# First expert tile in four lots beside the second tile's input projection

## The chip, the cores and the metric

One core of one Trainium2 chip runs the whole program. The metric is the device time of one execution in microseconds. The kernel before takes 2155.31 us, the median of three runs (2154.33 to 2156.59).

## The reference, cut to what matters

A model of two blocks works on 256 tokens of width 1024, in float32. The first block has two layers. Each layer is a mixer (attention) followed by a feed-forward part that retrieves experts by product keys, a chunk of 128 tokens at a time:

```
q = (xc @ w_q).reshape(t, PEER_HEADS, 2, PEER_QDIM // 2)
sc = jnp.einsum('thpc,hpnc->thpn', q, sub_keys)
v_half, i_half = lax.top_k(sc, 16)
cand = v_half[:, :, 0, :, None] + v_half[:, :, 1, None, :]
top_s, pos = lax.top_k(cand.reshape(t, 8, -1), 16)
g = softmax(top_s)
act = gelu(einsum('thkd,td->thk', u_tab[expert], xc))
out = einsum('thk,thkd->td', g * act, v_tab[expert])
```

Each token picks 8 heads x 16 = 128 experts. Each expert is a row of u and a row of v, 8 KB together. With 128 tokens on 128 partitions, one pick (say, head 3, rank 5) of all tokens is one gather of 1 MB. There are 128 such gathers for each tile of 128 tokens and each layer, 512 in all. The second block has four kinds of attention, gates and an MLP, and gathers nothing.

## The kernel before, in words

The tokens are two tiles of 128. The program is a list of stages. `stage` (L273) adds one, and `run_stages` (L278) has PE, ACT and DVE run their part of each and meet at its end (the wait at L289). The stages of the first layer are: the mixer of tile 0 (`hybrid(0)`), the feed-forward norm, turn and routing of tile 0 (`feed_forward(0, [0], enter_hybrid, halved=True)`, L1643), the mixer of tile 1, and the feed-forward of tile 1.

Routing (`route`, L1319) has three steps. PE makes the queries in four blocks of 512 columns (L1359). ACT copies them out (L1383). PE multiplies each block with the keys of two heads (L1348), and ACT copies the scores out (L1378). DVE then finds the 16 best of each of 16 score lists (`top16`, L1403, rounds of MAX8, FIND_INDEX8 and MATCH_REPLACE8) and, in `select` (L1431), combines the two halves of each head, takes the 16 best pairs and turns their places into expert numbers (L1436 to L1488). For tile 0 of the first layer this runs in two lots of four heads (`halved`), and the first lot's numbers go to POOL before the second lot is sorted. The softmax over the picks is a subtraction on DVE (L1503), an exp on ACT (L1393) and three DVE instructions (L1506 to L1508), once for all heads, at the end of the stage.

Beside that routing, after the query blocks and key scores, PE runs the input projection of tile 1 (`enter_hybrid`, L1198): eight transposes (L1216), and six column blocks in two halves each (L494). Its first four column blocks read weights that were kept in SBUF since tile 0. Those eight kept pieces lie in the eight slots of the ring into which the gathers land, so gather n (n below 8) waits until PE has read piece n (L2611). ACT empties the blocks (L1038).

POOL issues the gathers in order (L2596 to L2615). From the ninth on, each waits until the slot's last use is over (`freed`, L1576).

The work on a gathered row is an item (`start_experts`, L1514). For item i, DVE takes the dot product of row i with the token (L1530). ACT makes gelu (L1546), the weight (L1547) and a diagonal matrix (L1555) of item i-1. PE adds row i-2 into `ps_acc` with two matmuls (L1566, four records), or DVE adds it (L1538), which `share_out` decides by the kind of the stage. Items are not a stage of their own: they are handed out at the `point`s of other stages (L256). Each point has a weight, and `handed_out` (L251) gives out items in proportion to the weight passed, so that 122 of the 128 are out when the next tile's routing ends:

```
return f["first"] + int(weight * min((P - HELD_BACK - f["first"]) / max(f["weight"], 1.0), RATE))
```

For the first tile's items, the points run from the rotations of tile 1 to the end of tile 1's routing. Their weights by stage are: rotations 25, turn 6, index 31, attention 53, turn 3, output projection 14.9, norm 9, turn 3, routing 92.5.

SP issues the weight loads in the order of `stream` (L2566 to L2577), each after the use that frees its slot of four.

## Time and profile before

| | us |
|---|---|
| median of three runs | 2155.31 |
| the profiled execution | 2154.64 |
| span of its trace | 2152.8 |
| outside the span | 1.8 |

| engine | busy us | share of the span |
|---|---|---|
| PE | 1669.8 | 78% |
| DVE | 1487.4 | 69% |
| ACT | 797.5 | 37% |
| POOL | 641.7 | 30% |

The span runs from the first instruction to the last. All positions below are us from its start. An engine's row in a timeline names the line, the operation, the output and inputs, and in brackets how long the engine was idle before and what ended the wait. Some fp32 matmuls show as two records.

### The profile page before, as it was taken

How to read it: one execution, taken by the hardware profiler on the slowest of the kernel's cores; microseconds unless marked ns; L12 is line 12 of the kernel's file. 1: busy time of each engine (PE TensorE's matmuls, PEld its weight loads, DVE VectorE, ACT ScalarE, POOL GpSimd, SP SyncE). 2: the span in 40 equal slices, each digit the busy share in tenths (PEclk: the TensorE clock that was granted, in tenths of full speed). 3: DMA queues.
4: the chain of work that ended last, by engine and by line, in shares of the span. 5: the costliest groups of instructions: out<-in, count | busy, mean ns of one | idle time of the engine just before them, and what ended most of it. 6: DMA issues, size and time to landing. Idle time of an engine off the chain costs nothing.

```text
span 2152.8 us, 20655 instructions
## 1 busy us (share of the span) xinstructions
PE 1669.8 (78%) x6494; PEld 1007.3 (47%) x6494; DVE 1487.4 (69%) x3088; ACT 797.5 (37%) x2066; POOL 641.7 (30%) x524
## 2 busy tenths in 40 slices
PE   8797777577767775777777487756777899898998
PEld 4573343522324353333344332544333465668986
DVE  4378867897666669876667897668777464566654
ACT  1213452234424322432452145113545343444542
POOL 0012444344433443543344364335454000000000
PEclk9999889889898887998889799887888999999999
DMA  7368999999999999999999999999999774474552
GB/s 273 144 233 349 398 392 421 419 419 422 415 421 388 401 421 389 418 420 421 396 381 414 385 399 422 420 421 421 367 413 406 302 279 173 176 293 147 181 191 98
DMA packets 105659, 745.29 MB, mean 346 GB/s; under 512 B 12880, under 2 KB 13520, under 8 KB 16720
## 3 DMA queue, kind: packets, MB, share of 16 engines
q0 software_dynamic: 73728, 536.90, 60.9%
q1 hardware_dynamic: 31248, 204.98, 24.7%
q10 hardware_dynamic: 576, 2.10, 0.3%
q8 instruction: 53, 0.87, 0.2%
q14 instruction: 54, 0.44, 0.1%
HBM read 742.89 MB, written 1.05 MB: 346 GB/s over the span
## 4 chain that ended last, share of the span: by engine, by line
PE 41%; DMA 21%; DVE 20%; ACT 10%; issue 6%; DVEq 1%; PEldq 1%; POOL 0%; PEld 0%; ACTq 0%; SPq 0%; POOLq 0%
DMA sb_work<-in_peer_uv,sb_expert 17%; PE ps_acc L1566 12%; PE bank L494 6%; DVE sb_work L1530 5%; PE bank L1359 4%; DVE sb_x L1538 3%; PE bank L2054 2%; DMA sb_wring<-in_peer_w_q 2%; ACT L1546 2%; PE bank L564 2%; PE ps_acc L564 2%; PE ps_acc L565 2%; PE ps_acc L566 2%; PE bank L775 2%; PE bank L565 2%
## 5 line engine op out<-in xcount | busy, mean ns | idle before, releaser
L2612 POOL DMA_INDIRECT sb_work<-in_peer_uv,sb_expert x512 | 638.7, 1247 | 1022.0 <-PE ps_acc L1566 473.4
L1566 PE MATMUL ps_acc<-sb_work,sb_diag 128*128 128x512 f32 x1304 | 689.6, 675 | 309.1 <-ACT sb_diag L1555 260.4
L1530 DVE CUSTOM_DVE_ANT_0 sb_work<-sb_work,sb_h 128x1024 f32<-128x1024 f32 x512 | 619.1, 1222 | 187.9 <-DMA sb_work<-in_peer_uv,sb_expert 180.0
L1566 PEld LDWEIGHTS ps_acc<-sb_work,sb_diag 128*128 128x128 f32 x1304 | 263.9, 215 | 678.0 <-issue 668.7
L1546 ACT ACTIVATE sb_dots<-sb_dots 128x1 f32<-128x1 f32 x512 | 102.3, 200 | 528.7 <-DVE sb_dots L1530 499.4
L1538 DVE SCALAR_TENSOR_TENSOR sb_x<-sb_work,sb_weight,sb_x 128x1024 f32<-128x1024 f32 x186 | 238.3, 1281 | 79.8 <-ACT sb_weight L1547 79.8
L558 DVE TENSOR_TENSOR sb_work_r<-sb_wring,sb_work_r 128x2048 fp32r<-128x2048 f32 (+1 forms) x76 | 138.2, 1840 | 118.3 <-ACT sb_work_r L551 118.1
L551 ACT CAST sb_work_r<-sb_wring 128x2048 fp32r<-128x2048 f32 (+1 forms) x76 | 115.4, 1545 | 117.8 <-PE ps_acc L566 44.1
L1547 ACT ACTIVATE sb_weight<-sb_dots,sb_share 128x1 f32<-128x1 f32 x512 | 150.8, 295 | 16.6
L1359 PE MATMUL bank<-sb_hT,sb_wring 128*128 128x128 f32 x1024 | 123.9, 285 | 23.4 <-DMA sb_wring<-in_peer_w_q 20.9
L1555 ACT ACTIVATE sb_diag<-sb_ident,sb_weight 128x128 f32<-128x128 f32 x326 | 130.9, 401 | 10.6
L1359 PEld LDWEIGHTS bank<-sb_hT,sb_wring 128*128 128x128 f32 x1024 | 122.0, 201 | 27.0 <-issue 25.7
L494 PE MATMUL bank<-sb_wring,sb_hT 128*128 128x512 f32 (+2 forms) x264 | 101.9, 543 | 19.9 <-DVEq L287 14.2
L1815 PE MATMUL bank<-sb_hT,sb_wring 128*128 128x128 f32 (+1 forms) x448 | 60.9, 305 | 33.2 <-issue 24.9
L494 PEld LDWEIGHTS bank<-sb_wring,sb_hT 128*128 128x128 f32 x264 | 48.2, 197 | 75.0 <-issue 70.4
L1815 PEld LDWEIGHTS bank<-sb_hT,sb_wring 128*128 128x128 f32 (+1 forms) x448 | 59.7, 200 | 35.1 <-issue 35.1
L565 PE MATMUL ps_acc<-sb_work_r 128*128 128x256 f32 (+1 forms) x224 | 74.6, 333 | 0.0
L2054 PE MATMUL bank<-sb_wring,sb_hT 128*128 128x512 f32 x128 | 58.7, 612 | 6.1 <-ACT sb_work L2062 4.6
L565 PE MATMUL bank<-sb_work_r 128*128 128x256 f32 (+1 forms) x192 | 61.5, 320 | 0.0
L494 PE MATMUL bank<-sb_work,sb_hT 128*128 128x512 f32 x128 | 58.9, 619 | 1.8 <-issue 0.9
L494 PE MATMUL bank<-sb_wring,sb_work 128*128 128x512 f32 x128 | 55.9, 595 | 2.0 <-DVEq L287 1.2
L775 PEld LDWEIGHTS bank<-sb_work,sb_probsT 128*128 128x128 f32 x336 | 46.3, 208 | 23.6 <-issue 14.7
(339 smaller groups left out, 2146.9 us busy)
## 6 DMA issues: line engine op xcount, KB each, us to landing
sb_wring<-in_w_mix SPq DMA_DIRECT2D x36, 1024.0 KB, 10.8
sb_wring<-in_peer_w_q SPq DMA_DIRECT2D x32, 1024.0 KB, 12.1
sb_wring<-in_w_gate SPq DMA_DIRECT2D x32, 1024.0 KB, 5.0
sb_wring<-in_w_up SPq DMA_DIRECT2D x16, 1024.0 KB, 5.1
sb_wring<-in_w_down SPq DMA_DIRECT2D x16, 1024.0 KB, 4.8
sb_wring<-in_mla_w_uq SPq DMA_DIRECT2D x12, 768.0 KB, 11.2
sb_work<-in_hyb_w_in SPq DMA_DIRECT2D x8, 1024.0 KB, 14.4
sb_wring<-in_hyb_w_out SPq DMA_DIRECT2D x8, 1024.0 KB, 8.8
```

The costliest lines, as they stand in the source:

```text
L494: last = e.matmul(u.ap[:, 0:bn], xT[:, k0 + k, t * P:(t + 1) * P], sl[:, k, b0:b0 + bn], start=k0 + k == 0, stop=k0 + k == chunks - 1)
L558: e.tensor_tensor(low, slot_ap(s)[:, k0:k0 + chunks, c0:c1], high, ALU.subtract).then_inc(lo_made.sem, 1)
L565: pe.matmul(ps, left[0], right[1], start=False, stop=False)
L1359: last = e.matmul(u.ap[:, j * P:(j + 1) * P], slot_ap(s)[:, k, j * P:(j + 1) * P], hT[:, k0 + k, t * P:(t + 1) * P], start=k0 + k == 0, st ...
L1530: e.tensor_tensor_reduce(u, u, h[:, t, :], 1.0, 0.0, ALU.mult, ALU.add, dots[:, i:i + 1]).then_inc(dot_ready, 1)
L1538: e.scalar_tensor_tensor(x[:, t, :], ring[:, n % RING, D:2 * D], weight[:, k:k + 1], x[:, t, :], ALU.mult, ALU.add).then_inc(slot_free[n % ...
L1546: link(e.activation(dots[:, k:k + 1], dots[:, k:k + 1], ACT.Gelu))
L1547: scaled = e.activation(weight[:, k:k + 1], dots[:, k:k + 1], ACT.Copy, scale=share[:, t, k:k + 1])
L1555: e.activation(diag[:, number % DIAGS, :], ident[:, :], ACT.Copy, scale=weight[:, k:k + 1]).then_inc(diag_ready, 1)
L1566: last = e.matmul(ps_acc[:, b * 512:(b + 1) * 512], diag[:, number % DIAGS, :], ring[:, n % RING, D + b * 512:D + (b + 1) * 512], start=k ...
L1815: last = e.matmul(u.ap[0:width, at:at + P], slot_ap(s)[:, k, c:c + width], hT[:, k0 + k, 0:P], start=k0 + k == 0, stop=k0 + k == DC - 1)
L2612: pool.indirect_dma_start(ring[:, n % RING, :], None, a["peer_uv"], bass.IndirectOffsetOnAxis(ap=expert[:, t, n % P:n % P + 1], axis=0)).t ...
```

## The change

1. The sorting code moves out of `route` into `top16` and `select`. `select` also takes a list of points and uses a part of the one-hot buffer of its own for each lot. The softmax becomes three functions, `lower_shares`, `raise_shares` and `weigh_shares`, which work on a lot of heads. Elsewhere `route` computes what it did, with one lot.
2. `enter_hybrid` and the `halved` routing go. A new stage, `open_experts`, takes their place for tile 0 of the first layer. It has four lots of two heads, and the shares of each lot are finished right after its selection.
3. The order on PE is: query block 0; transposes of tile 1 with key scores 0 between them; query block 1; projection blocks 1 to 4 with key scores 1 after the first half; query block 2; projection block 5 with key scores 2 in its middle; query block 3; projection block 6 with key scores 3 in its middle. The scaling of the transposed tile 1 moves from ACT to two DVE instructions ahead of the first sort.
4. The first tile's items start in this stage. The lots after the first carry 18 points each of weight 0.85, one after each step of the sort.
5. The item with k = 0, 32, 64 or 96 waits on ACT for its lot's shares. POOL waits for a new lot of numbers at every 32nd gather (the loop at L2596 is as before).
6. The two weight pieces of query block 3 no longer pass through the slots. They are loaded into `mixed` and `probs`, which are idle then, by SP ahead of the pieces of query block 1, once the turn of tile 0's mixed heads is done.
7. The key scores of this stage go to the bank `ps_scores`.

The core of the diff:

```diff
+        def load_guests(free_from):
+            def load(sp):
+                for e in ("dve", "act", "pe"):
+                    sp.wait_ge(done[e], free_from)
+                for (view, chunks, cols), place, landed in zip(guests, guest_places, guest_landed):
+                    sp.dma_start(place[:, 0:chunks * cols], view).then_inc(landed, 16)
+        def open_experts():
+            lots = [range(2 * b, 2 * b + 2) for b in range(4)]
+            first_at = (0, 0, 0, 0, 3, 6, 9, 12, 14)
...
+            plan_queries(0)
+            asides[SLOTS] = keys_loads.pop(0)
+            asides[plan[0][0][1][0] + 1] = load_guests(mixed_turned[0])
+            start_experts(0, 0)
+            feeds[-1]["shares"] = weighed
+            with_queries = {0: 1, 4: 2, 5: 3}
...
+            for b in range(1, 4):
+                late.append([point(0.85) for _ in range(18)])
+                feeds[-1]["limits"].append((feeds[-1]["weight"], 2 * TOP * b))
...
+                def between(e, i, half):          # PE, after each half of a projection block
+                    if (i, half) == (0, 0):
+                        score(1)
+                    for p in late[0][first_at[2 * i + half]:first_at[2 * i + half + 1]] if i < 4 else ():
+                        p("pe", e)
+                    if i == 3 and half:
+                        queries(2, [late[0][14 + j:15 + j] for j in range(4)])
+                    if i == 4 and half == 0:
+                        score(2)
+                    if i == 4 and half:
+                        for p in late[1][0:4]:
+                            p("pe", e)
+                        queries(3, [late[1][4 + 3 * j:7 + 3 * j] for j in range(4)])
...
+                def between(e, i):                # ACT, after it emptied a projection block
+                    if i == 0:
+                        take_scores(e, key_units[1], 1)
+                        raise_lot(0)
...
+                    if i == 3:
+                        for p in late[0][14:18]:
+                            p("act", e)
+                        take_queries(e, plan[2][1], 2)
+                        raise_lot(1)
+                        take_scores(e, key_units[2], 2)
...
+            def dve(e):
...
+                for b, lot in enumerate(lots):
+                    key_units[b].wait_emptied(e)
+                    points = late[b - 1] if b else []
+                    top16(e, halves[4 * b:4 * b + 4], points[0:5])
+                    select(e, 0, 0, lot, picked[b], points[5:])
+                    lower_shares(e, 0, lot)
+                    weigh_shares(e, 0, lot, raised[b], weighed[b])
@@ def act(e, i):  (in start_experts)
+                    if f["shares"] and k % (P // len(f["shares"])) == 0:
+                        e.wait_ge(shares_ready.sem, f["shares"][k * len(f["shares"]) // P])
@@
-        def feed_forward(layer, tiles, beside=None, halved=False):
+        def feed_forward(layer, tiles):
+            if (layer, tiles) == (0, [0]):
+                open_experts()
+                return
-        feed_forward(0, [0], enter_hybrid, halved=True)
-        start_experts(0, 0)
+        feed_forward(0, [0])
```

## Rows read from the trace of the kernel before

**Rows 1.** The page, second part: GB/s in 40 slices of 53.8 us.

```profile
GB/s 273 144 233 349 398 392 421 419 419 422 415 421 388 401 421 389 418 420 421 396 381 414 385 399 422 420 421 421 367 413 406 302 279 173 176 293 147 181 191 98
```

**Rows 2.** Busy time by windows: length, then each engine's busy us (instructions), clock, DMA share, GB/s.

```profile
99.00:146.00 47.00, 45.93 (x321) 39.76 (x322) 28.04 (x131) 7.96 (x21) 0.00 (x0) 0.96 0.41 153
146.00:185.00 39.00, 29.86 (x77) 14.61 (x76) 35.41 (x156) 8.86 (x22) 7.67 (x8) 0.91 0.82 323
200.00:250.00 50.00, 39.43 (x116) 17.72 (x116) 38.70 (x81) 20.86 (x64) 22.98 (x21) 0.99 1.01 422
250.00:325.00 75.00, 57.17 (x198) 32.11 (x195) 54.86 (x86) 41.59 (x121) 29.30 (x26) 0.80 0.95 384
400.00:518.00 118.00, 77.44 (x259) 39.98 (x258) 107.15 (x298) 39.49 (x126) 49.73 (x41) 0.87 1.01 420
```

**Rows 3.** Timeline of POOL: start us, us, gathers number 0, 8, 9 and 127.

```profile
146.34 1.09 POOL L2612 DMA_INDIRECT sb_work<-in_peer_uv,sb_expert  x1 [144.09 <-DVE sb_expert L1488]
...
185.34 1.08 POOL L2612 DMA_INDIRECT sb_work<-in_peer_uv,sb_expert  x1 [21.22 <-PE ps_acc L1566]
187.06 1.42 POOL L2612 DMA_INDIRECT sb_work<-in_peer_uv,sb_expert  x1 [0.64 <-PE ps_acc L1566]
...
514.14 0.94 POOL L2612 DMA_INDIRECT sb_work<-in_peer_uv,sb_expert  x1 [2.52 <-PE ps_acc L1566]
```

**Rows 4.** Timeline of DVE: two item dots, with two more between them.

```profile
518.53 1.27 DVE L1530 CUSTOM_DVE_ANT_0 sb_work<-sb_work,sb_h 128x1024 f32<-128x1024 f32 x1 [1.11 <-DMA sb_work<-in_peer_uv,sb_expert]
...
525.99 1.23 DVE L1530 CUSTOM_DVE_ANT_0 sb_work<-sb_work,sb_h 128x1024 f32<-128x1024 f32 x1 [1.26 <-DMA sb_work<-in_peer_uv,sb_expert]
```

**Rows 5.** Groups of 175.5 to 518.5 us: count, busy us, mean ns, idle before.

```profile
L2612 POOL DMA_INDIRECT sb_work<-in_peer_uv,sb_expert x120 | 145.4, 1212 | 205.6 <-PE ps_acc L1566 135.1 <-DVE sb_x L1538 63.0 <-issue 7.5
L1530 DVE CUSTOM_DVE_ANT_0 sb_work<-sb_work,sb_h 128x1024 f32<-128x1024 f32 x123 | 148.5, 1223 | 28.0 <-DMA sb_work<-in_peer_uv,sb_expert 26.7
```

**Rows 6.** Timeline of SP: the loads of that stretch, first issue, us to the last.

```profile
335.01 53.99 SPq L2577 DMA_DIRECT2D sb_wring<-in_peer_w_q  x8
...
407.11 6.86 SPq L2577 DMA_DIRECT2D sb_wring<-in_mla_w_in  x4
```

**Rows 7.** Timeline of PE, 99 to 163 us.

```profile
99.17 16.24 PE L1359 MATMUL bank<-sb_hT,sb_wring 128*128 128x128 f32 x128 [0.79 <-ACTq L287]
...
116.13 7.36 PE L1359 MATMUL bank<-sb_hT,sb_wring 128*128 128x128 f32 x64
123.33 1.06 PE L1348 MATMUL bank<-sb_keys,sb_work 128*128 128x128 f32 x8
...
133.26 1.04 PE L1216 MATMUL ps_turn<-sb_ident,sb_h 128*128 128x128 f32 x8
135.20 27.70 PE L494 MATMUL bank<-sb_work,sb_hT 128*128 128x512 f32 x64 [0.90 <-issue]
```

**Rows 8.** Timeline of ACT: the first query copy, and the exp of the shares.

```profile
108.29 0.59 ACT L1383 COPY sb_work<-bank 128x512 f32<-128x512 f32 x1 [7.39 <-PE bank L1359]
...
172.52 0.33 ACT L1038 COPY sb_work<-bank 128x200 f32<-128x200 f32 x1 [2.06 <-PE bank L494]
172.86 1.28 ACT L1393 ACT_TABLE_LOAD   x1
174.16 0.31 ACT L1393 ACTIVATE sb_share<-sb_share 128x128 f32<-128x128 f32 x1
```

**Rows 9.** Timeline of DVE: one round of sorting and one selection of four heads.

```profile
125.11 0.87 DVE L1412 MAX8 sb_probsT<-sb_work 128x8 f32<-128x128 f32 x4 [2.84 <-ACT sb_work L1378]
...
130.46 0.23 DVE L1436 CAST sb_probsT<-sb_probsT 128x128 f32<-128x128 uint32 x1
...
140.80 1.22 DVE L1484 TENSOR_REDUCE sb_probsT<-sb_work 128x64 f32<-128x1024 f32 x1
...
145.83 0.23 DVE L1488 SCALAR_TENSOR_TENSOR sb_expert<-sb_probsT 128x64 int32<-128x64 f32 x1
```

**Rows 10.** Records of L1566 on PE, 250 to 275 us: ns min/median/max.

```profile
L1566 PE MATMUL ps_acc<-sb_work,sb_diag x20: 592/592/1192, 258.8 to 271.3; 128*128 128x512 f32 x20
```

More of the change, by code:

```diff
@@ L480, in project_parts @@
                     given_back[s] = last_use
-            points = [point(len(tiles) * chunks * bn * 0.0017, "pe") for _, _, bn, _, _, _ in plan]
+            points = [point(len(tiles) * chunks * bn * 0.0017, "pe") if pointed else (lambda name, e: None)
+                      for _, _, bn, _, _, _ in plan]
             def pe(e, between=None, turned=None):
@@ L1316, in load_keys, with top16, end_round @@
             return load
-        def route(layer, t, beside=None, halved=False):
-            lots = [range(0, EH // 2), range(EH // 2, EH)] if halved else [range(EH)]
+        def top16(e, items, after=()):
+            link = chains["dve"]
+            after = list(after)
+            def end_round():
+                link.wait()
+                if after:
+                    after.pop(0)("dve", e)
+            for v, m, at in items:
+                link.add(e.max(m[:, 0:8], v))
+            end_round()
+            for v, m, at in items:
+                link.add(e.max_index(at[:, 0:8], m[:, 0:8], v))
+            end_round()
+            for v, m, at in items:
+                link.add(e.match_replace(v, m[:, 0:8], v, TAKEN))
+            end_round()
+            for v, m, at in items:
+                link.add(e.max(m[:, 8:16], v))
+            end_round()
+            for v, m, at in items:
+                link.add(e.max_index(at[:, 8:16], m[:, 8:16], v))
+            end_round()
@@ new lines, in weigh_shares @@
+        def weigh_shares(e, t, lot, raised, ready=None):
+            link = chains["dve"]
+            h0, n = lot[0], len(lot)
+            sh = share[:, t, h0 * TOP:(h0 + n) * TOP].rearrange("p (h k) -> p h k", h=n)
+            total = small[:, 240 + h0:240 + h0 + n]
+            e.wait_ge(from_act.sem, raised)
+            link(e.tensor_reduce(total, sh, AX.X, ALU.add))
+            link(e.reciprocal(total, total))
+            last = e.tensor_tensor(sh, sh, total.unsqueeze(2).to_broadcast([P, n, TOP]), ALU.mult)
+            if ready:
+                last.then_inc(shares_ready.sem, 1)
+            else:
+                link(last)
@@ L1332, in route @@
             key_units.append(products.take())
[L1333 to L1337 removed]
+            if layer and t == 0:
+                asides[plan[0][0][0][0]] = keys_loads.pop(0)
+            lowered, raised = to_act.plan(), from_act.plan()
+            picked = experts_ready.plan()
+            routed[layer, t] = [picked]
             made = [point(7.0, "pe") for _ in range(4)] + [point(7.0, "pe")]
@@ L1583, in share_out @@
             for f in feeds:
+                for behind, limit in f["limits"]:
+                    assert handed_out(f, behind) <= limit
                 f["adder"], f["number"], f["before"] = [], [], []
```

361 lines of the change are left out of this document (205 added, 156 removed).

## The prediction

> **What bounds the kernel now.** Start with the page's slices [rows 1]. From the fifth to the thirty-first slice the DMA engines mostly move 415 to 422 GB/s, never under 367. Nowhere else is that rate reached. So through the four tiles of gathers the kernel waits for bytes, and what counts is how early they start and how seldom they pause. The table by windows shows the pauses around the change [rows 2]: 153 GB/s in 99 to 146 us and 323 in 146 to 185, against 422 in 200 to 250. The timeline of POOL says why [rows 3]: gather 0 goes out at 146.34, right after the first lot's numbers. Gathers 1 to 7 follow as the ring comes free. Gather 8 must wait until 185.34, when the first item has been added, because items are handed out only after all sorting. From 185.34 to 514.14 gathers 8 to 127 pass, 120 of them [rows 3, 5].
>
> The price of a gather when DMA is the limit comes from the dots that wait for rows: 518.53 to 525.99 are three steps, so 7.46/3 = 2.49 us for 1 MB [rows 4]. Gathers 8 to 127 and the twelve weight loads of that stretch [rows 6] are 132 MB, 329 us at this price. 185.34 + 329 = 514.1, and gather 127 is issued at 514.14. The agreement is partly luck, as the last gathers issued have yet to land, but DMA is the limit of the stretch. DVE is not far behind. It is busy 107.15 of 118 us in 400 to 518 [rows 2].
>
> So a change ahead of 185 us is worth this: the time at which gathers run freely moves later or earlier, and each gather issued beforehand takes 2.49 us off what is left.
>
> **The change, part by part.** First comes PE's order. The first query block is copied out at 108.29, as now [rows 8]. Transposes 1.04, key scores 1.06 and query block 1 at 7.36 [rows 7] follow: 108.2 + 9.5 = 117.7. DVE waits about 1 us for the transposes, scales them and starts lot 0 at about 111, against 117 now.
>
> A lot costs DVE one round of sorting and one selection of two heads. The round is 125.11 to 130.46 = 5.35 us [rows 9]. A selection of four heads runs from 130.46 to the end of its last step at 146.06 = 15.6. Six of its steps are on 128x1024 operands, as the one at 140.80, at 1.22 and a gap of 0.04, 7.6 in all, and the rest is 8.0. For two heads the bounds are half (7.8) and the whole (15.6). The wide steps go with their width and I take 0.72 each. The rest are narrow steps, and only some have half as many, so I take 5.7. That gives 10.0, nearer to half. All selections together then take 40 us in place of 31.
>
> So lot 0's numbers are ready at 111 + 15.4 = 126.6, some 20 us before 146.34. Lot 0's shares need a table load and an exp on ACT, 1.28 + 0.31 [rows 8], and three small steps. DVE is through at about 129.5, lot 1 with six dots at 1.2 [rows 5] at about 153.
>
> Now lot 2 needs scores from PE. From 117.7 PE does four projection blocks (27.70) and key scores 1 (1.06), which is 146.5. Four items are added between them, at 1.72 each by the spacing of gathers 8 and 9, which go at PE's pace [rows 3]: 6.9. PE waits twice for a diagonal matrix, an estimate of 4.7, since ACT handles an item only after emptying the block that PE is just finishing. Then come query block 2 (7.36), half a block (3.46), key scores 2 (1.06) and the copy (0.59). Sum: 170.6. DVE stands idle from about 153 to 170.6, because ACT's exp for lot 1 is queued behind the copy of query block 2 and the scores of lot 2 come later still.
>
> Lots 2 and 3 are DVE's: each 15.35 + 0.25 + about 1.6 for the exp + 0.65 = 17.9, and 14 dots at 1.23 make 17.2. Sum 52.9, so the stage ends at 223.4. Bounds: 219 with no wait on PE and the selection at 9.5; 228 with the selection at 11 and PE items at 1.9. If nothing waited for PE it would be 206. The same stage ends at about 175.5 now.
>
> The items follow from the weights. The old sum is 237.4 and the rate 122/237.4 = 0.514. The new sum is 237.4 + 54 x 0.85 + 1 = 284.3 and the rate 0.429. At the end of the stage 20 items are out, 18 added by PE, and 26 gathers issued. With the next stage PE adds item 18's row (k = 18) at once, so gather 26 goes at 223.4 + 1.8 = 225.2. This is the state that now holds at 185.34 for gather 8. Hence 225.2 - 185.3 = 39.9 later, and 18 gathers ahead, 18 x 2.49 = 44.8: **a gain of 4.9 us**.
>
> Something goes back. DVE's own work after the stage is the same, while its slack shrinks. With 20 items fewer, 50 us of DMA time leave the free run but only 20 x 1.22 = 24 us of DVE time, and some 6 us of adds move from DVE to PE; of the 28.0 us that DVE waits for rows now [rows 5] about 8 are left. DVE also starts the rotations only 2 us before the free run, now 10 us before. So in the rotations and at the start of the index stage the ring runs dry for a while, as DMA has no backlog. I put it at 3 us, between 0 (the smaller bursts in the attention stage, which moves 384 GB/s now [rows 2], win something) and 8 (that stage's loss once more: (422-384)/422 x 75 = 6.8). Net: 1.9 us less.
>
> The rest costs nothing where its cover holds. The two extra-early loads (2 MB, 5 us) are issued at about 84 us, when PE has 14 us of other work, and 99 to 146 moves only 153 GB/s [rows 2]; without cover query block 0 would be late by up to 5. Four exps for one are three table loads more, and three more back to gelu, 6 x 1.28 = 7.7 us on ACT, busy 8.86 of 39 us [rows 2]; only the exp halves are on DVE's path, counted above. The wait for shares at k = 0 is over before the dot. POOL's wait for lots 1 to 3 is never last: gather 32 is issued after the stage. Later tiles route as now, so past gather 127 all moves rigidly with the gathers.
>
> **A rule against the change.** The trace shows the load of a table for 1.28 us, starting 0.01 us after the copy before it ended and followed by the exp within 0.02 [rows 8]. The Trainium skill, "ScalarE: Activation LUTs", section "What ACT_TABLE_LOAD costs", adds a drain of about 1.38 us to each switch, and its section "Table sets: the hidden batching unit" asks that calls be batched by set, against which four lots sin. By the page three exps more would cost DVE 4 us more than by the row. The row shows no such drain, and the row stands.
>
> **Rivals.**
> *A, nothing holds DVE.* If lot 2's scores came by 153, the stage would end at 206 and the gain be 4.9 + 17 - 3 = 19: 2136. For it: PE has 45.93 of 47 busy now, and nothing slower is asked. Against: PE's sum above has little that could fall out. 12%.
> *B, the give-back is none or a gain.* Fewer items in each group of attention fill the ring of eight more evenly, and half of the 6.8 us lost there comes back: 4.9 + 3.4 = 8.3, 2147. For it: a point of that stage has weight 6, which is 3.1 items now and 2.6 then. Against: DVE has less slack. 23%.
> *C, slower by PE's clock.* PE now runs back to back until 172, with the clock at 0.96 [rows 2]. In the new stage it waits for diagonals and shares its time with DVE. Where it did so later, in 250 to 325, it was busy 57 of 75 us at a granted 0.80 [rows 2], and a record of L1566 takes 592 ns or 1192 ns [rows 10], at the clock's two levels, 2.4 and 1.2 GHz. From 139 to 170 PE has some 27 us of work ahead of lot 2's scores, 34 at 0.80: 7 later, and the items and waits of lots 2 and 3 add some 2. Then 2153.4 (below) + 9 = 2162.4. It decides against the change once the stage ends after about 225.3, and shows beyond 0.2% after 229.6. 20%.
> *D, it does not do what it says.* The ring takes rows early, but the rows past the eighth come so late (gather 8 only at PE's first item) that fewer than 18 are ahead; three fewer cost 7.5: 2160.9. 5%.
>
> **The numbers.** The forecast, no change that can be told, 2154.64 - 1.9 = 2152.7 for an execution like the profiled one. The profiled one is 0.7 under the median of 2155.31, so the median to expect is 2153.4. What can be told from no change is 0.2%, 4.3 us. Forecast 40%, its own range 2150 to 2158; faster is A and B, 35%; slower is C and D, 25%. The range from 2143 to 2164 holds B, D and the most of C with an error of 2 or 3 us, and leaves out A and a slower clock still.
>
> **What would show it.** Gather 0 at 127 and the end of the stage (the first rotation on DVE) at 219 to 228. DVE idle for 15 to 18 us ahead of lot 2's MAX8. 26 gathers by then. Gather 127 at 508 to 516. If DVE's idle time is under 5 us, A is right; if the granted clock in 140 to 225 is under 0.85 with records at 1192 ns, C. Wrong would be above all a wait between the lots that is not in this list, or a free run with DMA at under 0.97 before 250.

## The result, and the profile after

The changed kernel takes 2160.28 us (median of 17 runs, 2153.92 to 2168.19) against 2155.31 us before (17 runs). The ratio is 1.0026, with a 95% interval of 1.0016 to 1.0035: 0.26% slower, some 5.6 us by the ratio and 5.0 by the medians. The profiled execution has a span of 2158.5 us against 2152.8, at the same granted clock (0.902, 0.900). The time lies in the wide range that was forecast (2143 to 2164), but outside the forecast's own 2150 to 2158, and on the other side of no change.

The page's slices of the changed kernel, to be read beside [rows 1], show only shifts from the tenth slice on. The second to fourth gain, the fifth, seventh and ninth lose:

```profile
GB/s 276 179 265 361 351 390 355 422 404 422 407 421 412 410 421 391 419 420 421 387 382 417 377 395 422 420 421 421 388 403 402 300 276 173 175 292 147 179 192 98
```

The timeline of POOL has gathers number 0, 25, 26, 127 and 128, to be read against [rows 3]:

```profile
126.77 1.09 POOL L2787 DMA_INDIRECT sb_work<-in_peer_uv,sb_expert  x1 [124.53 <-DVE sb_expert L1408]
...
220.15 1.94 POOL L2787 DMA_INDIRECT sb_work<-in_peer_uv,sb_expert  x1 [6.22 <-PE ps_acc L1737]
225.83 0.94 POOL L2787 DMA_INDIRECT sb_work<-in_peer_uv,sb_expert  x1 [3.75 <-PE ps_acc L1737]
...
520.67 0.94 POOL L2787 DMA_INDIRECT sb_work<-in_peer_uv,sb_expert  x1 [1.42 <-PE ps_acc L1737]
525.07 0.94 POOL L2787 DMA_INDIRECT sb_work<-in_peer_uv,sb_expert  x1 [3.46 <-PE ps_acc L1737]
```

Gather 0 goes out 19.6 us earlier than before. Gather 26 goes at 225.83, where gather 8 went at 185.34: 40.5 later and, at 2.49 us for each of 18 gathers, 44.8 ahead, by that price a gain of 4.3. Gather 128, the first of the second tile, comes at 525.07. Before the change it was this:

```profile
518.54 0.94 POOL L2612 DMA_INDIRECT sb_work<-in_peer_uv,sb_expert  x1 [3.46 <-PE ps_acc L1566]
```

That is 6.5 later, so 10.9 us were given back between gathers 26 and 128. From there on both kernels do the same (5.7 us apart in span).

Where it went is in the table by windows, after the change [rows 2, for before]:

```profile
99.00:146.00 47.00, 43.72 (x210) 29.53 (x211) 35.43 (x166) 9.00 (x19) 6.75 (x6) 0.96 0.59 227
146.00:185.00 39.00, 35.92 (x163) 22.13 (x162) 20.60 (x86) 11.99 (x33) 9.34 (x9) 1.00 0.82 296
200.00:250.00 50.00, 37.08 (x81) 14.70 (x82) 46.25 (x145) 19.24 (x58) 20.76 (x18) 0.90 0.91 369
250.00:325.00 75.00, 58.23 (x195) 28.43 (x193) 57.66 (x106) 38.31 (x109) 32.91 (x27) 0.91 0.98 383
325.00:400.00 75.00, 57.20 (x172) 28.15 (x173) 49.45 (x84) 29.03 (x86) 30.83 (x24) 0.89 0.96 374
400.00:518.00 118.00, 81.49 (x371) 51.65 (x369) 108.25 (x309) 32.64 (x111) 52.49 (x39) 0.87 1.00 413
```

and the same view of the kernel before, for the one stretch that is not among [rows 2]:

```profile
325.00:400.00 75.00, 55.43 (x244) 34.30 (x243) 53.33 (x95) 20.00 (x65) 33.15 (x25) 0.89 1.01 420
```

Against 421 GB/s, 325 to 400 now loses (421-374)/421 x 75 = 8.4 us (0.2 before). But these windows hold other stages in the two kernels. Cut at the same events, the stretch splits into four: from gather 8 (26 after the change) to attention's first scores, attention, its end to the second tile's first query block, and from there to gather 128. First the kernel before, then the changed one:

```profile
185.34:249.43 64.09, 53.52 (x147) 23.59 (x145) 53.02 (x120) 25.69 (x82) 33.21 (x29) 1.00 0.98 405
249.43:328.13 78.70, 60.62 (x204) 33.64 (x205) 56.69 (x89) 43.56 (x125) 31.72 (x27) 0.80 0.95 386
328.13:373.64 45.51, 32.97 (x81) 13.90 (x81) 31.94 (x50) 13.89 (x43) 19.80 (x16) 0.89 1.01 421
373.64:518.54 144.90, 97.56 (x415) 59.66 (x416) 126.72 (x339) 44.60 (x144) 60.65 (x49) 0.87 1.01 420
```

```profile
225.83:285.74 59.91, 48.88 (x134) 21.08 (x133) 52.59 (x127) 24.41 (x78) 32.06 (x26) 1.00 0.96 375
285.74:356.85 71.11, 52.87 (x192) 28.89 (x193) 47.83 (x77) 40.00 (x112) 27.95 (x22) 0.83 0.96 375
356.85:398.23 41.38, 31.57 (x77) 13.33 (x77) 28.51 (x45) 12.71 (x38) 17.12 (x15) 0.92 0.99 384
398.23:525.07 126.84, 87.95 (x395) 55.42 (x396) 114.06 (x321) 38.51 (x123) 55.33 (x42) 0.88 1.01 414
```

Against 421 GB/s the four lost 2.4, 6.5, 0.0 and 0.3 us before, and lose 6.5, 7.8, 3.6 and 2.1 now. The new losses are 4.1, 1.2, 3.6 and 1.8, together 10.7 of the 10.9 us.

The groups of 221 to 526 us say what VectorE waited for (columns as in [rows 5]), and below them the same view of the kernel before has its adds in 175 to 519:

```profile
L1699 DVE CUSTOM_DVE_ANT_0 sb_work<-sb_work,sb_h 128x1024 f32<-128x1024 f32 x105 | 126.0, 1222 | 5.3 <-DMA sb_work<-in_peer_uv,sb_expert 3.9 <-ACTq L288 0.3
L1707 DVE SCALAR_TENSOR_TENSOR sb_x<-sb_work,sb_weight,sb_x 128x1024 f32<-128x1024 f32 x28 | 35.9, 1282 | 20.5 <-ACT sb_weight L1718 20.5
```

```profile
L1538 DVE SCALAR_TENSOR_TENSOR sb_x<-sb_work,sb_weight,sb_x 128x1024 f32<-128x1024 f32 x34 | 43.6, 1282 | 8.9 <-ACT sb_weight L1547 8.9
```

The waits for rows fell to 3.9 us (26.7 in [rows 5]), more than forecast. In their place stand 20.5 us of waits for weights from ScalarE, where 8.9 stood.

In the open stage VectorE's timeline shows the idle time ahead of lot 2, and then the first rotation, which is the stage's end:

```profile
167.22 0.19 DVE L1435 TENSOR_REDUCE sb_small<-sb_share 128x2 f32<-128x32 f32 x1 [15.33 <-ACT sb_share L1425]
...
170.00 0.87 DVE L1325 MAX8 sb_probsT<-sb_work 128x8 f32<-128x128 f32 x4 [2.17 <-ACT sb_work L1533]
...
221.90 0.42 DVE L716 TENSOR_TENSOR sb_probs<-sb_work,sb_cos 128x256 f32<-128x256 f32 x1 [0.62 <-ACTq L288]
```

### The profile page after: what moved, and what is told of

It reads as the page before. It is cut to its first block, busy times and chain, and to the rows that moved or that the text cites. A ratio compares the mean times of both kernels' runs of the same rounds, so it can differ in the third digit from the quotient of the medians.

```text
span 2158.5 us, 20800 instructions
## 1 busy us (share of the span) xinstructions
PE 1685.7 (78%) x6518; PEld 1012.1 (47%) x6518; DVE 1489.5 (69%) x3148; ACT 804.9 (37%) x2073; POOL 656.1 (30%) x524
## 4 chain that ended last, share of the span: by engine, by line
PE 41%; DVE 22%; DMA 19%; ACT 10%; issue 6%; DVEq 1%; PEldq 1%; POOL 0%; PEld 0%; SPq 0%; ACTq 0%; POOLq 0%
DMA sb_work<-in_peer_uv,sb_expert 15%; PE ps_acc L1737 12%; PE bank L522 6%; DVE sb_work L1699 6%; PE bank L1521 4%; DVE sb_x L1707 4%; PE bank L2229 2%; DMA sb_wring<-in_peer_w_q 2%; ACT L1717 2%; PE bank L592 2%; PE ps_acc L592 2%; PE ps_acc L594 2%; PE ps_acc L593 2%; PE bank L593 2%; PE bank L594 2%
## 5 line engine op out<-in xcount | busy, mean ns | idle before, releaser
L2787 POOL DMA_INDIRECT sb_work<-in_peer_uv,sb_expert x512 | 652.0, 1273 | 1010.6 <-PE ps_acc L1737 467.6
L1737 PE MATMUL ps_acc<-sb_work,sb_diag 128*128 128x512 f32 x1328 | 706.7, 678 | 305.9 <-ACT sb_diag L1726 257.6
L1737 PEld LDWEIGHTS ps_acc<-sb_work,sb_diag 128*128 128x128 f32 x1328 | 269.1, 215 | 683.4 <-issue 671.2
L1707 DVE SCALAR_TENSOR_TENSOR sb_x<-sb_work,sb_weight,sb_x 128x1024 f32<-128x1024 f32 x180 | 230.5, 1281 | 93.5 <-ACT sb_weight L1718 93.5
L1521 PE MATMUL bank<-sb_hT,sb_wring 128*128 128x128 f32 x960 | 118.1, 288 | 25.0 <-DMA sb_wring<-in_peer_w_q 22.4
L1726 ACT ACTIVATE sb_diag<-sb_ident,sb_weight 128x128 f32<-128x128 f32 x332 | 133.3, 402 | 10.9
L1521 PEld LDWEIGHTS bank<-sb_hT,sb_wring 128*128 128x128 f32 x960 | 116.4, 204 | 29.4 <-issue 28.3
L1990 PE MATMUL bank<-sb_hT,sb_wring 128*128 128x128 f32 (+1 forms) x448 | 59.8, 301 | 30.7 <-issue 15.8
L838 ACT COPY sb_probsT<-ps_turn 128x512 f32<-128x512 f32 (+2 forms) x48 | 23.9, 533 | 87.7 <-PE ps_turn L789 87.6
```

What stands on the lines that cost most here:

```text
L1521: last = e.matmul(u.ap[:, j * P:(j + 1) * P], slot_ap(s)[:, k, j * P:(j + 1) * P], hT[:, k0 + k, t * P:(t + 1) * P], start=k0 + k == 0, st ...
L1707: e.scalar_tensor_tensor(x[:, t, :], ring[:, n % RING, D:2 * D], weight[:, k:k + 1], x[:, t, :], ALU.mult, ALU.add).then_inc(slot_free[n % ...
L1726: e.activation(diag[:, number % DIAGS, :], ident[:, :], ACT.Copy, scale=weight[:, k:k + 1]).then_inc(diag_ready, 1)
L1737: last = e.matmul(ps_acc[:, b * 512:(b + 1) * 512], diag[:, number % DIAGS, :], ring[:, n % RING, D + b * 512:D + (b + 1) * 512], start=k ...
L1990: last = e.matmul(u.ap[0:width, at:at + P], slot_ap(s)[:, k, c:c + width], hT[:, k0 + k, 0:P], start=k0 + k == 0, stop=k0 + k == DC - 1)
L2787: pool.indirect_dma_start(ring[:, n % RING, :], None, a["peer_uv"], bass.IndirectOffsetOnAxis(ap=expert[:, t, n % P:n % P + 1], axis=0)).t ...
```

## The experiments

Each was timed beside the kernel before. "End" is the first rotation, "behind" the items of the first tile that are left for the stretch behind the open stage, "picks" the end of the second tile's last selection step, "length" the time from the end to the picks. Times in us. The positions are those of one profiled execution of each kernel, and its time can lie some us beside the kernel's median (6.4 below it in heavy_after, 4.1 above it in thin92_before), so differences of 1 or 2 us in the table say little.

| kernel | end | behind | length | picks | gather 128 | ratio to before (95%) |
|---|---|---|---|---|---|---|
| before | 175.6 | 122 | 336.9 | 512.5 | 518.5 | 1 |
| heavy_before | 176.1 | 122 | 337.5 | 513.6 | 519.7 | 1.0003 (0.9991 to 1.0015) |
| thin_before | 176.6 | 102 | 298.5 | 475.0 | 527.8 | 1.0042 (1.0028 to 1.0057) |
| thin92_before | 174.8 | 92 | 290.6 | 465.4 | 541.0 | 1.0109 (1.0095 to 1.0124) |
| no_items | 192.4 | 122 | 339.9 | 532.2 | 538.3 | 1.0077 (1.0063 to 1.0091) |
| early_no_items | 186.3 | 122 | 338.5 | 524.8 | 531.0 | 1.0071 (1.0056 to 1.0086) |
| after | 221.9 | 102 | 296.8 | 518.6 | 525.1 | 1.0026 (1.0016 to 1.0035) |
| no_guests | 223.0 | 102 | 297.2 | 520.3 | 526.7 | 1.0030 (1.0017 to 1.0042) |
| late_weigh | 221.8 | 102 | 298.5 | 520.2 | 526.4 | 1.0032 (1.0018 to 1.0047) |
| heavy_after | 222.3 | 102 | 299.3 | 521.6 | 528.9 | 1.0044 (1.0026 to 1.0061) |
| dense_mixer | 221.6 | 102 | 311.9 | 533.5 | 541.2 | 1.0094 (1.0078 to 1.0110) |
| hole_items | 227.2 | 98 | 298.4 | 525.6 | 532.6 | 1.0043 (1.0029 to 1.0056) |
| early_queries | 216.3 | 102 | 299.8 | 516.1 | 522.9 | 1.0020 (1.0008 to 1.0032) |
| late_items | 221.5 | 102 | 298.2 | 519.6 | 526.0 | 1.0027 (1.0011 to 1.0043) |
| late_items14 | 204.2 | 107 | 306.6 | 510.7 | 518.5 | 0.9999 (0.9988 to 1.0009) |
| early_adds | 212.1 | 102 | 297.6 | 509.7 | 516.1 | 0.9992 (0.9980 to 1.0005) |
| early_adds14 | 199.5 | 107 | 308.0 | 507.5 | 515.1 | 0.9979 (0.9968 to 0.9989) |
| pe_adds_before | 175.5 | 122 | 349.4 | 524.9 | 531.0 | 1.0069 (1.0053 to 1.0085) |
| pe_adds_after | 223.1 | 102 | 307.2 | 530.2 | 538.3 | 1.0096 (1.0077 to 1.0115) |
| pe_adds_best | 202.2 | 107 | 317.4 | 519.6 | 527.0 | 1.0035 (1.0025 to 1.0045) |

**Is it the thinner mixer?** In thin_before one number of the kernel before is altered (26; 36 in thin92_before):

```
-   return f["first"] + int(weight * min((P - HELD_BACK - f["first"]) / max(f["weight"], 1.0), RATE))
+   held_back = 26 if f is feeds[0] else HELD_BACK
+   return f["first"] + int(weight * min((P - held_back - f["first"]) / max(f["weight"], 1.0), RATE))
```

> The kernel before the change with one number altered: the second tile's mixer and routing hand out 102 items of the first tile instead of 122 (0.43 per unit of weight instead of 0.514, the density of the changed kernel), and the remaining ones stand behind the routing. The open stage is that of the kernel before. The theory of the thin mixer: the holes that the changed kernel shows at 300 to 380 us appear here too, 45 us earlier; the first dot of the second tile comes 8 to 11 us later than 518.5, and the total rises by 8 to 11 us to 2163 to 2166. The rival, that density costs nothing because the ring of eight keeps the transfers fed either way: the stages become shorter by what is taken out, the DMA makes it up, and the total stays within 2 us of 2155.

Measured 8 to 9 us, the lower end of the first theory: the open stage is that of before, and the thin mixer alone brings a loss of the size of the give-back. The length falls by 38.4 us for 20 items, 1.9 each.

no_items takes the items out of the changed kernel's open stage:

```
-            start_experts(0, 0)
-            feeds[-1]["shares"] = weighed
...
         feed_forward(0, [0])
+        start_experts(0, 0)
```

> The changed kernel with no expert in the open stage: its four lots, its order and its guests stay, and the experts are handed out from the end of the stage on, with 0.51 items per unit of weight as before the change. Leaves the 20 dots of the stage for later. The theory of the thin mixer: without items the stage ends at about 195 (175.5 before the change, because lots 0 and 1 of VectorE still wait for the order of TensorE), everything behind it is as in the kernel before, moved by that difference of 19 us: first dot of the second tile at about 538, total about 2174, and the GB/s behind the stage as in the kernel before. The rival, that the give-back comes from what the stage does to the start of the free run whatever the density: the same stage end, and the first dot of the second tile another 8 to 11 us later, total about 2184.

End 192.4, gather 128 at 538.3: the first theory. With 122 items behind it, the stretch takes 339.9, as before the change (336.9) and not 8 to 11 more.

dense_mixer gives the mixer its density back and thins the routing (the weight of each point of route is multiplied by `less`):

```
-                late.append([point(0.85) for _ in range(18)])
+                late.append([point(0.72) for _ in range(18)])
...
+            less = 0.575 if (layer, t) == (0, 1) else 1.0
```

> The changed kernel with the weights of the points shifted: the points of the open stage 0.72 instead of 0.85 and those of the second tile's routing at 0.575 of theirs, so that 20 experts still stand in the open stage, and the mixer of the second tile hands out 0.51 items per unit of weight, as before the change, instead of 0.43; the routing of the second tile hands out fewer. The theory that the thinner mixer lets the DMA queue run dry: the DMA of 300 to 380 us (336 to 382 GB/s in the changed kernel) comes back to above 400 GB/s, the first dot of the second tile comes 5 to 9 us earlier than 525.1, and the total falls by 5 to 9 us, to 2151 to 2155. The rival, that VectorE has no time left in these stages and the hole only moves to the routing: GB/s of 300 to 380 rise, those of 400 to 518 fall, and the total stays within 2 us of 2160. A second rival, that the loss lies right behind the open stage (230 to 280 us): within 2 us as well, with 300 to 380 us unchanged in shortfall.

All three missed: 20 us slower than before, 15 slower than the changed kernel. The windows show how:

```profile
250.00:325.00 75.00, 54.38 (x157) 24.35 (x156) 58.75 (x108) 37.48 (x113) 29.39 (x27) 0.93 1.01 413
325.00:400.00 75.00, 58.86 (x198) 30.75 (x196) 43.98 (x72) 28.00 (x84) 29.48 (x24) 0.87 0.91 354
400.00:530.00 130.00, 85.31 (x389) 54.15 (x390) 106.80 (x314) 34.16 (x108) 47.26 (x38) 0.87 0.95 382
```

The start fills up (413, after 383), but 325 to 400, where attention ends, falls to 354 (374 in the changed kernel), and the routing, where VectorE has its own sorting whatever the items, now asks for too few rows (382, 413 in the changed kernel). What the mixer's start won didn't make up for what the later stages lost.

**Who bounds the stretch?** Ten reductions are added to VectorE in each of the two kernels:

```
+                if n0 == 0 and i in range(30, 110, 8):
+                    e.tensor_reduce(extra[:, :], h[:, t, :], AX.X, ALU.add)
```

> The kernel before with ten extra reductions of 1.2 us on VectorE, one after every eighth dot of the first tile from item 30 to item 102, 12.2 us in all; the output stays the same. The theory that before the change VectorE had slack in these stages (27.8 us of waits for rows): gather 128 comes 3 to 7 us later than 518.5 and the total rises by no more than 7 us, to 2162 or less. The rival, that VectorE's sum bounded this stretch before as well: +11 to +13 us, 2167.

> The changed kernel with the same ten reductions on VectorE, 12.2 us in all. The theory that since the change VectorE's own sum bounds the stretch (3.9 us of waits for rows): nearly all of it shows, gather 128 9 to 13 us later than 525.1, total 2169 to 2173. The rival, that the loss of the change lies in the DMA and VectorE has as much slack as before: the same rise as in the kernel before, 3 to 7 us.

In the kernel before 12.1 us of VectorE work cost nothing that can be told (gather 128 comes 1.2 us later), less than even the first theory wanted. In the changed one they cost some 4 us by the medians, with intervals that overlap, 2.5 in length and 3.8 at gather 128, as the rival said, not 9 to 13. So my theory that VectorE's sum is now the bound fell. These are VectorE's waits by line, for rows and for weights, in heavy_before (175 to 520) and in heavy_after (222 to 529): line, releaser, total us, times, longest. In heavy_before they replace 27.8 and 8.9, in heavy_after 3.9 and 20.5:

```profile
DVE sb_work L1531 <- DMA sb_work<-in_peer_uv,sb_expert: 19.4, 22, 1.7
DVE sb_x L1541 <- ACT sb_weight L1550: 7.7, 3, 3.7
```

```profile
DVE sb_x L1710 <- ACT sb_weight L1721: 16.6, 4, 5.2
...
DVE sb_work L1700 <- DMA sb_work<-in_peer_uv,sb_expert: 0.7, 2, 0.4
```

thin92_before asks where the length stops to fall:

> The kernel before with 92 items of the first tile handed out in the second tile's mixer and routing (122 before, 102 in thin_before). It asks where the stretch from the first rotation to the second tile's picks stops to shrink: 336.9 us with 122 items, 298.5 with 102. The theory of a floor, that with 102 items the stages' own chains through ScalarE and TensorE already bound it: 290 to 297 us with 92, and ten gathers more behind it at 2.49 us, total 17 to 25 us above thin_before's 2162.6. The rival, 2.0 us an item all the way down: 278 us, total 5 us above thin_before.

The floor is there, softer than stated: 7.9 us for ten items (0.8 each), where 122 to 102 brought 1.9 to 2.0. The total, 15.9 us above thin_before, stays just under the 17 to 25 of the theory. Attention shows the floor best: with 28 dots in it, it took 78.7 us, with 23 in thin_before 69.6, and with 20 here 71.7, at granted clocks of 0.80, 0.85 and 0.81.

(Attention is counted here from its first scores on TensorE to the first turn of its result.) To see if the waits for weights make the floor, each third item of attention was left to TensorE like the others (pe_adds_after is the changed kernel with it, pe_adds_before the kernel before, pe_adds_best early_adds14, which is told below):

```
-    plan.append(g | value | {"points": [point(6.0, "both"), point(6.0, "both")]})
+    plan.append(g | value | {"points": [point(6.0, "dve" if len(feeds) == 1 else "both") for _ in range(2)]})
```

> The changed kernel with one thing altered in the second tile's attention: every item there is added by TensorE, where now each third (k%3 == 2) is added by VectorE. Such an add waits for the item's weight from ScalarE, which at every point first does its own four exps; VectorE has waited 20.5 us for that in six places since the change (6.79 at 309.51, 4.71 at 326.16), against 8.9 us in four before it. The theory that these waits make the floor under the stretch behind the open stage: 12 to 15 us of waits and 7 or 8 adds of 1.28 go from VectorE, the stretch to gather 128 shortens by 6 to 14 us from 303.2 and the total is 2147 to 2155. The rival, that the attention is bound by its own chain of scores, exps and turns, in which VectorE merely stands at another place: less than 3 us, total 2158 to 2161.

> The same edit in the kernel before, where the rows are the limit of the stretch (27.8 us of waits for rows on VectorE): gather 128 and the total within 2 us of 518.5 and 2155. The rival, that the waits of the adds cost as much there: 4 to 8 us faster.

> The same edit in early_adds14, the version below both kernels so far (2149.6), which waits 18.6 us for weights and 12.4 us for rows in the stretch. Theory: the stretch to gather 128 shortens by 4 to 8 us from 315.6, less than in the changed kernel, since rows are partly the limit, and the total is 2142 to 2146. The rival: less than 2 us, 2148 to 2150.

All missed, in the other direction (the last three rows of the table). Attention, with seven adds more on TensorE (nine in the kernel before), takes 80.8 us instead of 71.1 in the changed kernel and 88.9 instead of 78.7 in the one before. This is the window of attention in pe_adds_after, to be read against 285.74 to 356.85 above:

```profile
287.12:367.95 80.83, 66.35 (x221) 35.24 (x221) 40.45 (x70) 41.75 (x118) 25.05 (x22) 0.85 0.86 329
```

VectorE has 7 us less to do and the stage is 10 longer. TensorE is busy 13.5 us more. In the changed kernel most of its idle time in attention is the following wait for diagonal matrices, which is 12.0 with the edit:

```profile
PE ps_acc L1737 <- ACT sb_diag L1726: 15.8, 4, 4.9
```

In pe_adds_after VectorE no longer waits for weights, but for rows:

```profile
DVE sb_work L1699 <- DMA sb_work<-in_peer_uv,sb_expert: 22.0, 13, 3.1
```

The rows are late because each gather there waits for TensorE's add of an earlier row (POOL waits 55.2 us for it in attention). So the length of attention is set by TensorE, with the diagonal matrices that ScalarE makes for it, and VectorE's waits for weights are only where its spare time shows.

**What does the open stage cost?** Several orders were tried. The first is early_queries, with query block 2 two projection blocks earlier, query block 3 one, and the weighing of lots 1 to 3 put off:

```
-            with_queries = {0: 1, 4: 2, 5: 3}
+            with_queries = {0: 1, 2: 2, 4: 3}
...
+                    if (i, half) == (1, 1):
+                        queries(2)
+                    if (i, half) == (2, 0):
+                        score(2)
...
-                    weigh_shares(e, 0, lot, raised[b], weighed[b])
+                    for at in {0: (0,), 3: (1, 2, 3)}.get(b, ()):
+                        weigh_shares(e, 0, lots[at], raised[at], weighed[at])
```

> The changed kernel with two things moved in the open stage: query blocks 2 and 3 of the first tile are multiplied after the second and fourth block of the projection instead of after the fourth and fifth, and the shares of lots 1 to 3 are weighed at the end of the stage, so that neither TensorE's order nor an exp behind a copy holds back lot 2. The theory that the DVE idle of 17.5 us ahead of lot 2 (15.33 and 2.17 us) is what turned the change into a loss: that idle goes, the first rotation comes at about 206 instead of 221.9, gather 26 at about 210 instead of 225.8, the give-back after it stays as it is (about 11 us against the pace of 2.49 us a gather), and the whole falls by 13 to 17 us from the changed kernel, to 2144 to 2148. The rival, that the transfers are the bound of this stretch as well: the stage ends at 206, but rows and weights then come later than they are wanted, and the total falls by no more than 6 us, to 2154 or more.

The end came at 216.3, not 206. The idle 17.5 us went, and 17.1 us of waits for rows came. The total, 2159.85 us, is not 13 to 17 lower but within the rival's limit. VectorE's longest, and POOL's gathers 4 and 6, say why:

```profile
161.89 1.23 DVE L1701 CUSTOM_DVE_ANT_0 sb_work<-sb_work,sb_h 128x1024 f32<-128x1024 f32 x1 [5.71 <-DMA sb_work<-in_peer_uv,sb_expert]
```

```profile
142.08 0.94 POOL L2789 DMA_INDIRECT sb_work<-in_peer_uv,sb_expert  x1 [9.64 <-PE bank L522]
...
156.48 0.94 POOL L2789 DMA_INDIRECT sb_work<-in_peer_uv,sb_expert  x1 [9.14 <-PE bank L522]
```

A gather waits until TensorE has used the projection weights that lie in its ring place, and those blocks now come behind the queries.

late_weigh has the put-off weighing alone:

> The changed kernel with one thing moved: the shares of lots 1 to 3 are raised and weighed at the end of the open stage, so that VectorE no longer waits 15.33 us for the exp of lot 1 behind the copy of query block 2. Scores 2, which VectorE needs next, are there at 170.0 either way, so nothing of the 17.5 us is won: the first rotation within 1 us of 221.9, the total within 2 us of 2160. The rival, that the exp was the real wait: lot 2 begins at 155 and the total falls by 10 us or more.

As expected, no gain (2163.0 us, a ratio whose interval overlaps that of the changed kernel): scores 2 are the real wait. hole_items puts more items into that wait, with the same edit and

```
-    late.append([point(0.85) for _ in range(18)])
+    late.append([point(0.85) for _ in range(18)] + [point(2.0) for _ in range(6 if b == 1 else 0)])
```

> late_weigh with five more items in the hole: six more points, of weight 2.0 each, after lot 1's selection on VectorE, where it waits for scores 2 from 153 to 170; TensorE and ScalarE come to them behind scores 2. About 24 instead of 20 items stand in the open stage, 98 instead of 102 behind it. The theory that since the change VectorE's own sum bounds the second tile's mixer and routing (it waits for rows 3.9 us there instead of 27.8), so that gather 128 comes when VectorE has done its work and not when the DMA has: the stage still ends at 221.9 within 2 us, each of the four or five items taken out of the stretch behind it shortens that by 1.6 us of work less some cover lost, gather 128 comes 2 to 6 us earlier than 525.1, total 2154 to 2158. The rival, that the thinner mixer is what costs: still fewer items in it open still more holes, gather 128 comes at 525 or later, total 2160 to 2163.

The rival was nearer, and worse than it said (1.0043). The items in the hole were not free: five waits for rows of 1.5 to 3.0 us stand between them, scores 3 then kept VectorE for 7.09 us, and the end moved to 227.2. With 98 items the length did not shrink at all (attention took 76.0 us at a granted clock of 0.75, against 71.1 at 0.83).

early_no_items is early_queries without items:

> early_queries with no expert in the open stage; they are handed out from its end on. It prices the order alone: without items VectorE has 59 us of own work from 110 on and waits neither for scores nor for rows, so that the stage ends at 174 to 178, where no_items took 192.4; the stretch behind it is that of the kernel before (337 to 340 us) and the total 2153 to 2158, about 15 us below no_items. The rival, that another wait (scores 2 or 3) takes its place: end at 185 or later, total 2163 or more.

End 186.3, the rival: scores 3 are late by 6.06 us. VectorE's own work from the first MAX8 on is 60.8 us here and 51.3 before the change, so four lots instead of two cost 9.5 us. The order costs 192.4 - 186.3 = 6.1.

late_items and late_items14 let no item stand beside lot 1 (points of 0.0, then 1.275 or 0.9):

> early_queries with its 20 experts of the open stage moved: none beside lot 1's selection, where VectorE waited 17.1 us for rows because the ring places come free only as TensorE is through the projection's kept weights, all 20 beside those of lots 2 and 3 (the points of lot 1 weigh 0, those of lots 2 and 3 1.275 instead of 0.85). The theory that the open stage was paid for by one wait or another (17.5 us for scores in the changed kernel, 17.1 us for rows in early_queries) and that the stretch behind it takes 297 to 300 us with 102 items whatever came before: the stage ends at 200 to 209, the picks of the second tile are ready at 499 to 508 (512.5 before the change, 518.6 after it), and the total is 2145 to 2152, less than in both kernels. The rival, that the rows can't come faster: the stage ends at 214 or later and the total stays at 2157 to 2161.

> The same with 14 instead of 20 items in the open stage (points of 0.9): the stage ends about 6 x 1.5 = 9 us earlier than in late_items, the stretch behind it holds 108 instead of 102 items and is, at 2.0 us each, 12 us longer. Theory: total 1 to 5 us above late_items. The rival, that the stretch has a slope of less than 1.5 us an item in this range: total below that of late_items.

The first missed: 221.5. VectorE had used the eight rows and waited 10.05 us, for TensorE's first add came at 173.06 and gather 8 at 177.08, 20.9 us after gather 7 was out. The second, with 15 items in the stage (its weights give 15, not 14), is as fast as the kernel before and 7.6 us below late_items. That is the rival's total but not its reason: the end moved by 17.3 us for five items and the length by 8.4, 1.7 each. early_adds and early_adds14 move the adds ahead, nine points beside query block 3 (on ScalarE behind block 4 of the projection) and four behind scores 3:

```
-    queries(3, [late[0][14 + j:15 + j] for j in range(4)])
+    queries(3, [late[0][14 + j:15 + j] + late[1][2 * j:2 * j + 2 + j // 3] for j in range(4)])
...
+    for p in late[0][14:18] + late[1][0:9]:
+        p("act", e)
```

> late_items with the first 13 of lot 2's points moved ahead on TensorE and ScalarE: nine of them stand beside query block 3's multiplication and ahead of its copy, four behind scores 3, instead of all 18 behind the fifth block of the projection. In late_items VectorE had used up the eight rows by 171 and waited 10.05 us for the next, because the first add, which frees a ring place, came at 173.06. The theory that this hole alone kept late_items from its forecast: first add at about 160, the wait of 10 us falls to 3 or less, the stage ends at 205 to 211 instead of 221.5, the stretch behind it takes 297 to 300 us, the picks are ready at 503 to 510 and the total is 2145 to 2152, below both kernels. The rival, that the rows then wait for something else (TensorE waits for the diagonals inside query block 3, scores 3 come late): the stage ends at 215 or later and the total is 2156 or more.

> The same order with 14 items in the open stage instead of 20 (points of 0.9). late_items14 ended its stage at 204.2, with 4 us of waits for rows in it. Theory: stage end at 197 to 201, 108 items behind it in 306 to 308 us, picks at 503 to 509, total 2147 to 2152. The rival as for early_adds: no gain over late_items14 (2154.8).

Both theories hold nearly: ends at 212.1 and 199.5, totals of 2152.27 and 2149.62 us. Here are, from the timelines of early_adds, TensorE's first add and gather 8, and then, of early_adds14, VectorE's only two waits for rows and the end:

```profile
160.08 1.88 PE L1743 MATMUL ps_acc<-sb_work,sb_diag 128*128 128x512 f32 x4
```

```profile
162.24 1.47 POOL L2793 DMA_INDIRECT sb_work<-in_peer_uv,sb_expert  x1 [5.72 <-PE ps_acc L1743]
```

```profile
190.64 1.23 DVE L1705 CUSTOM_DVE_ANT_0 sb_work<-sb_work,sb_h 128x1024 f32<-128x1024 f32 x1 [0.33 <-DMA sb_work<-in_peer_uv,sb_expert]
...
194.38 1.23 DVE L1705 CUSTOM_DVE_ANT_0 sb_work<-sb_work,sb_h 128x1024 f32<-128x1024 f32 x1 [1.17 <-DMA sb_work<-in_peer_uv,sb_expert]
...
199.46 0.42 DVE L716 TENSOR_TENSOR sb_probs<-sb_work,sb_cos 128x256 f32<-128x256 f32 x1 [0.21 <-issue]
```

early_adds14 is faster than both kernels, by 0.21% (0.11 to 0.32) than the one before. early_adds can't be told from the kernel before. The last five items cost more than they bring: from 15 to 20 the end moves 12.7 later and the length shrinks by 10.4.

no_guests loads query block 3 through the slots:

> The changed kernel with the weights of query block 3 loaded through the ring of four slots as before the change, instead of into the two idle buffers. They, and all weights after them, are then loaded when earlier slots come free. The theory that this part of the change is worth little here: stage end 221 to 225, total 2160 to 2164. The rival, that TensorE then waits for weights in the stage: stage end at 228 or later and total 2166 or more.

As expected, 1.1 us at the end and no measurable difference.

## Why the prediction was wrong

**The open stage was right.** Gather 0 at 127 (126.77), lot 2 at 170.6 (170.00), 17.6 us of idle (17.5), the end at 223.4 (221.90), 26 gathers, gather 26 at 225.2 (225.83), the gain at this point 4.9 (4.3). The clock was 1.00 in 146 to 185 and 0.94 in 140 to 225, so rival C had no part. Rivals A and D did not occur either; A's 206 was not to be had by taking the wait on TensorE away, as early_queries shows, since the rows then come late.

**The step that failed is the give-back: "I put it at 3 us, between 0 and 8".** It was 10.9. The sum paid 2.49 us for each gather ahead, the price while DMA is the limit, and took 3 off for what VectorE lacks. But the way to gather 128 became shorter by 34.0 us (333.2 from gather 8, 299.2 from gather 26), not by the 44.8 of 18 gathers, and from the end of the stage to the picks 20 items fewer are worth 40.1 us (336.9 to 296.8), 2.0 each. DMA stops to be the limit in parts of the mixer: VectorE's waits for rows fell from 27.8 to 3.9, against the 8 that I forecast (I had also read the group's whole idle time, 28.0, as waits for rows, which are 26.7 of it), and DMA paused instead. thin_before has a loss of this size (8 to 9 us) without the rest of the change, and no_items, with the rest of the change and 122 items behind its open stage, has a length only 3.0 above that of before. In the terms that the runs measured, the end of the stage moves by +9.5 for four lots, +1.2 for what else early_no_items has (longer waits and more short gaps, less an earlier start), +6.1 for the order and +29.5 for 20 items in the stage (1.5 each, against no_items). With -40.1 behind it, that is +6.2 at the picks (6.1 by the rows; the sum closes because its terms are differences of the same rows).

**The reason given for it was only half right.** I put it down to VectorE's slack and to the restart after the stage. The restart is seen, and is the largest piece: 4.1 us up to attention, where I had 3 for all. DMA's share there was 0.94 from 225.83 to 250, under the 0.97 that I had named as a sign of being wrong, and gather 127 came at 520.67, not at 508 to 516. The other 6.6 us I had put at nothing or at a gain. Attention, where my bound of 8 lay, lost only 1.2 more, but what stands behind it up to the second tile's queries lost 3.6 and the routing 1.8, and I named neither. And VectorE had slack: 12.1 us more cost it 2.5 to 4. The attention stage is paced from TensorE's side, which pe_adds shows in both kernels.

**Rival B** (fewer items fill the ring more evenly) is refuted by thin_before. The table loads did not decide: VectorE's waits for the exps of lots 0, 2 and 3 are 1.30, 0.29 and 0.29 us.

**What stays open.** No run took away one wait of TensorE's chain in attention. The trace puts 15.8 us of it to the diagonals from ScalarE (15.6 before the change), but whether these, TensorE's matmuls or its clock would shorten the stage most was not tried. That attention does not get shorter below 23 dots is seen in one execution of thin92_before, at another granted clock. Why the two stages behind attention pause more is not shown either.

## What to carry to other kernels

Work moved out of a stretch is worth what that stretch gets shorter by, and that must be read for the density it has afterwards: a price taken while one resource is the limit holds only as long as it is. Measure the slope with one number altered (thin_before) before building the order that needs it. And where a wait is taken away in a stage that also frees buffers, look first at what is released later by the new order: here scores, then ring places, then adds were next in line, each for 10 us or more, until the order of all three was changed together.

## What was not expected of the hardware

An add takes TensorE about twice as long at its lower clock, and attention runs there part of the time in each version (its granted clock is 0.75 to 0.88). Two of its adds in the changed kernel, four records each, from the timeline of PE, the first at a granted clock of 1.00 (320 to 324), the second at 0.50 (339 to 344):

```profile
321.21 1.98 PE L1737 MATMUL ps_acc<-sb_work,sb_diag 128*128 128x512 f32 x4
...
339.94 3.75 PE L1737 MATMUL ps_acc<-sb_work,sb_diag 128*128 128x512 f32 x4 [4.85 <-ACT sb_diag L1726]
```

VectorE's add takes 1.28 us in all 28 cases, whatever TensorE's clock. Handing seven of them to TensorE cost 10 us of attention, 1.4 each, in a stage in which TensorE was busy 74% and VectorE 67% of the time.
